# Small experts of a mixture-of-experts layer: more weights split in two, folded and shorter row transfers, and a halved last chunk

## The reference

```
def moe_ffn(h, router_w, router_b, w1, w3, w2):
    logits = h @ router_w + router_b
    top_v, top_i = lax.top_k(logits, 2)
    top_w = jax.nn.softmax(top_v, axis=-1)
    combine = jnp.sum(jax.nn.one_hot(top_i, 8) * top_w[..., None], axis=-2)
    y = jnp.zeros_like(h)
    for e in range(8):
        y = y + combine[..., e:e+1] * swiglu(h, w1[e], w3[e], w2[e])
    return y
```

## Time and profile before

| what | value |
|---|---|
| median of 3 runs (lowest, highest) | 1486.67 us (1479.36, 1486.76) |
| the profiled execution: time, span | 1481.48 us, 1479.8 us |
| granted TensorE clock, mean | 0.993 |
| busy share of the span: PE, DVE, ACT, POOL | 97%, 83%, 64%, 7% |
| moved by DMA | 496 MB, mean 335 GB/s |

### The profile page before, as it was taken

One profiled execution on the slowest core, in us unless ns is written; L12 is line 12 of the kernel. 1 busy time (PEld: TensorE's weight loads), 2 busy tenths in 40 slices (PEclk: granted clock), 3 DMA queues, 4 the chain that ended last, 5 costly groups with the idle time before them and its releaser, 6 DMA issues.

```text
span 1479.8 us, 18836 instructions
## 1 busy us (share of the span) xinstructions
PE 1441.7 (97%) x7449; PEld 1147.2 (78%) x7449; DVE 1233.4 (83%) x1183; ACT 941.4 (64%) x877; POOL 97.8 (7%) x156
## 2 busy tenths in 40 slices
PE   8999999999999999999999999999999999999897
PEld 4886699999988748888887877887867887776674
DVE  5887888887886388998988989888979888988787
ACT  3533444444564247777787877787877787876766
POOL 5400100000000021010000010000010000000000
PEclk9999999999999999999999999999999999999899
DMA  9867588888853349999999999999999999999993
GB/s 348 307 228 284 198 323 320 301 301 303 300 185 115 114 170 333 369 391 379 383 352 374 407 402 410 397 402 409 411 402 409 398 402 409 410 402 410 397 403 154
DMA packets 162436, 496.21 MB, mean 335 GB/s; under 512 B 4650, under 2 KB 8918, under 8 KB 162342
## 3 DMA queue, kind: packets, MB, share of 16 engines
q1 hardware_dynamic: 156160, 474.76, 83.8%
q0 software_dynamic: 5504, 18.78, 3.8%
q10 hardware_dynamic: 678, 1.40, 0.2%
HBM read 483.91 MB, written 11.01 MB: 334 GB/s over the span
## 4 chain that ended last, share of the span: by engine, by line
PE 71%; DMA 12%; DVE 11%; ACT 2%; issue 2%; SPq 1%; POOL 0%; DVEq 0%; ACTq 0%
DMA ring<-in_moe_w_dram 11%; PE bank L1451 9%; PE bank L1452 9%; PE bank L1453 9%; DVE ring_low L2250 6%; PE bank L1091 5%; PE bank L1449 4%; PE bank L1450 4%; PE bank L1299 4%; PE bank L1340 3%; PE bank L1339 3%; PE bank L1338 3%; PE bank L1088 3%; PE bank L1494 2%; PE bank L1314 2%
## 5 line engine op out<-in xcount | busy, mean ns | idle before, releaser
L2250 DVE TENSOR_TENSOR ring_low<-ring,w_high 128x2048 fp32r<-128x2048 f32 x237 | 537.4, 2290 | 53.0 <-ACT w_high L2792 49.4
L2792 ACT ACTIVATE w_high<-ring 128x2048 fp32r<-128x2048 f32 x237 | 451.4, 1920 | 125.2 <-DMA ring<-in_moe_w_dram 60.5
L2250 DVE TENSOR_TENSOR ring_low<-ring,xn_high 128x2048 fp32r<-128x2048 f32 x79 | 180.9, 2289 | 13.7 <-ACT xn_high L2792 11.9
L2705 ACT ACTIVATE tmp_r<-ring 128x1024 fp32r<-128x1024 f32 x84 | 89.0, 1061 | 140.8 <-PE bank L1340 81.9
L1452 PE MATMUL bank<-ring_low,x_high 128*128 128x512 f32 x448 | 175.8, 392 | 0.0
L2792 ACT ACTIVATE xn_high<-ring 128x2048 fp32r<-128x2048 f32 x79 | 151.3, 1915 | 33.7 <-DMA ring<-in_moe_w_dram 18.7
L1450 PE MATMUL bank<-ring_low,x_high 128*128 128x512 f32 x400 | 156.9, 392 | 0.0
L1451 PE MATMUL bank<-w_high,x_high 128*128 128x512 f32 x336 | 133.3, 397 | 0.0
L2046 DVE TENSOR_TENSOR ring_low<-ring,tmp_r 128x1024 fp32r<-128x1024 f32 x84 | 102.6, 1225 | 34.7 <-ACT tmp_r L2705 33.0
L1453 PE MATMUL bank<-w_high,x_low 128*128 128x512 f32 x336 | 131.1, 390 | 0.0
L1449 PE MATMUL bank<-w_high,x_high 128*128 128x512 f32 x304 | 124.2, 408 | 4.7 <-DVE ring_low L2250 3.9
(11 more groups left out here) (448 smaller groups left out, 2619.3 us busy)
## 6 DMA issues: line engine op xcount, KB each, us to landing
ring<-in_moe_w_dram SPq DMA_DIRECT2D x168, 2048.0 KB, 17.1
ring<-in_w_mod_dram SPq DMA_DIRECT2D x23, 2048.0 KB, 13.0
ring<-in_ffn_w_dram SPq DMA_DIRECT2D x21, 2048.0 KB, 11.8
ring<-in_w_in_dram SPq DMA_DIRECT2D x7, 2048.0 KB, 14.1
ring<-in_w_out_dram SPq DMA_DIRECT2D x4, 2048.0 KB, 8.5
ring<-in_w_in_dram SPq DMA_DIRECT2D x4, 1024.0 KB, 15.5
expert_rows<-act_low POOLq DMA_DIRECT2D x5, 512.0 KB, 6.1
ring<-in_w_mod_dram SPq DMA_DIRECT2D x2, 1024.0 KB, 16.1
```

Source lines behind the costliest of these rows:

```text
L2250: tt_(moe_low(u, m // 2)[:, c], moe_slot(u, m // 2)[:, c], high_place(q, g, u, m).bitcast(F32), ALU.subtract).then_inc(low_made, 1)
L2792: act(high_place(q, g, u, m), moe_slot(u, m // 2)[:, c], ACT.Copy).then_inc(high_made, 1)
```

## The change

Four edits:

- `PLAIN` is empty: all units of small experts are split. Only unit 40 of the last expert (`LAST_PLAIN`) stays whole, in `last_down`.
- The last chunk of the last expert is loaded as two transfers of 1 MB with a semaphore each, so that PE can start on unit 40 when its half is there.
- `row_gate` of a small expert adds the two halves of its rows on DVE (two additions of 64 x 512, `fold_v`), and `rows_out` then writes 64 rows by one scatter. The index lists, the adding scatter and the clearing of the spare rows go.
- `tokens_in` gathers 64 rows for small experts, and `turn_rows` transposes 64.

```diff
-PLAIN = (4,16,23,33,39,)
+PLAIN = ()
+LAST_PLAIN = (UNITS - 2,)
...
         def is_plain(q, g, u, m):
-            return is_small(q, g, u) and m in PLAIN
+            return is_small(q, g, u) and (m in PLAIN or (is_last(q, g, u) and m in LAST_PLAIN))
...
-                    eng.dma_start(dst, src).then_inc(landed[(NPRE + c) % RING], 16)
+                    if q == 0 and c == NE * NCH - 1:
+                        eng.dma_start(dst[:, 0:HB // 2, :], src[:, 0:HB // 2, :]).then_inc(s_last_half, 16)
+                        eng.dma_start(dst[:, HB // 2:, :], src[:, HB // 2:, :]).then_inc(landed[(NPRE + c) % RING], 16)
+                    else:
+                        eng.dma_start(dst, src).then_inc(landed[(NPRE + c) % RING], 16)
...
-            for n in range(2 * TT + 1):
+            for n in range(2 * TT):
                 eng.dma_start(expert_rows[n * P:(n + 1) * P, :], y_low.bitcast(F32)).then_inc(s_zero, 16)
...
-                if is_small(0, g, u):
-                    eng.indirect_dma_start(expert_rows[:, :],
...
-                    eng.wait_ge(s_rows_out, 16 * (rows_before(r) + 1))
-                    eng.indirect_dma_start(expert_rows[:, :],
...
-                                           compute_op=ALU.add).then_inc(s_rows_out, 16)
...
+                n = SMALL if is_small(0, g, u) else SLOTS
+                eng.indirect_dma_start(expert_rows[:, :],
+                                       bass.IndirectOffsetOnAxis(index[0:n, g % 2, 0, u, u:u + 1], 0),
+                                       rows_place(r)[0:n, :], None, bounds_check=2 * T + P - 1,
+                                       oob_is_err=False).then_inc(s_rows_out, 16)
...
+                                if is_plain(q, g, u, m):
+                                    ins = mm(bank[4 + half][:, :], act_high[:, j % 2, h].bitcast(F32),
+                                             moe_slot(u, i).rearrange("p (b n) -> p b n", n=D)[:, hb, c],
+                                             start=False, stop=hb == HB - 1)
+                                    continue
...
+                done(eng, tt_(rows[:, c], bank[4 + half][:, :], gate_row[:, c],
+                              ALU.mult).then_inc(fold_v.sem, 1), fold_v, f"y{half}", small_rep(r // PAIR, r % PAIR))
+                done(eng, tt_(rows[0:SMALL, c], rows[0:SMALL, c], rows[SMALL:SLOTS, c],
+                              ALU.add).then_inc(row_v.sem, 1), row_v, f"y{half}", r)
...
-                for u in range(PAIR):
-                    done(eng, tt_(index_f[:, u, PAIR:], index_f[:, u, u:u + 1].to_broadcast([P, 2]), own_rows,
-                                  ALU.max).then_inc(index_v.sem, 1), index_v, f"s{u}", g)
```

More of the change, by code:

```diff
@@ L137 @@
 N_CONSTS = 86
-LATE_CONSTS = 5 + LATER
+LATE_CONSTS = 2 + LATER
 UNUSED = 1000.0
@@ L151 @@
 assert all(COPY_NAMES.index(f"p{j}") < COPY_NAMES.index(f"q{j}") for j in range(NJ))
-SPLITS = [(n, m) for n in range(NE) for m in range(UNITS) if not (n in SMALL_AT and m in PLAIN)]
+LAST_PLAIN = (UNITS - 2,)
+SPLITS = [(n, m) for n in range(NE) for m in range(UNITS)
+          if not (n in SMALL_AT and m in PLAIN) and not (n == NE - 1 and m in LAST_PLAIN)]
 SPLIT = {unit: n for n, unit in enumerate(SPLITS)}
@@ L270 @@
     "index_v":
-        ("f s0 s1 t i").split(),
+        ("f t i").split(),
     "row_v":
+        ("y0 y1").split(),
+    "fold_v":
         ("y0 y1").split(),
@@ L673, in split_at @@
         def split_at(q, g, u, m):
[L675 to L679, removed]
+            if q:
+                return len(SPLITS) + (g * PAIR + u) * UNITS + m + 1
+            return SPLIT[g * PAIR + u, m] + 1
         def high_place(q, g, u, m):
@@ L692, in rows_before @@
         def rows_before(r):
-            return r + sum(is_small(0, n // PAIR, n % PAIR) for n in range(r))
+            return r
         def halves_of(j):
@@ L969, in tokens_in @@
                 for u in range(PAIR):
-                    eng.indirect_dma_start(xn[:, u, :], None, token_rows[:, :],
-                                           bass.IndirectOffsetOnAxis(index[:, g % 2, 1, u, PAIR:PAIR + 1], 0),
+                    n = SMALL if is_small(0, g, u) else SLOTS
+                    eng.indirect_dma_start(xn[0:n, u, :], None, token_rows[:, :],
+                                           bass.IndirectOffsetOnAxis(index[0:n, g % 2, 1, u, PAIR:PAIR + 1], 0),
                                            bounds_check=T - 1, oob_is_err=False).then_inc(s_gathered, 16)
@@ L1401, in turn_rows @@
                         c = k % 2 * T + u * P
-                        ins = nc.tensor.transpose(b[:, c:c + P], xn[:, u, k * P:(k + 1) * P], ident)
+                        rows = SMALL if is_small(0, rep, u) else SLOTS
+                        ins = nc.tensor.transpose(b[:, c:c + rows], xn[0:rows, u, k * P:(k + 1) * P],
+                                                  ident[0:rows, 0:rows])
                 mark(ins.then_inc(gather_t.sem, 1), gather_t, f"g{n}")
@@ L1443, in units_made @@
                         return
-                    moe_arrived(eng, q, g, u, m // 2)
+                    if is_last(q, g, u) and m in LAST_PLAIN:
+                        eng.wait_ge(s_last_half, 16)
+                    else:
+                        moe_arrived(eng, q, g, u, m // 2)
                 def three(out_, x_h, x_l, w_h, w_l, first, last):
@@ L2263, in row_gate @@
                     eng.wait_ge(s_rows_out, 16 * rows_before(r))
-                done(eng, tt_(rows_place(r)[:, half * W:(half + 1) * W], bank[4 + half][:, :], gate_row[:, half * W:(half + 1) * W],
-                              ALU.mult).then_inc(row_v.sem, 1), row_v, f"y{half}", r)
+                c = slice(half * W, (half + 1) * W)
+                rows = rows_place(r)
+                if not is_small(0, r // PAIR, r % PAIR):
+                    done(eng, tt_(rows[:, c], bank[4 + half][:, :], gate_row[:, c],
+                                  ALU.mult).then_inc(row_v.sem, 1), row_v, f"y{half}", r)
+                    return
+                done(eng, tt_(rows[:, c], bank[4 + half][:, :], gate_row[:, c],
+                              ALU.mult).then_inc(fold_v.sem, 1), fold_v, f"y{half}", small_rep(r // PAIR, r % PAIR))
+                done(eng, tt_(rows[0:SMALL, c], rows[0:SMALL, c], rows[SMALL:SLOTS, c],
+                              ALU.add).then_inc(row_v.sem, 1), row_v, f"y{half}", r)
             def indices(g):
```

27 lines of the change are left out of this document (6 added, 21 removed).

## The result

The changed kernel takes 1488.01 us (median of 20 runs, 1480.81 to 1490.90), the kernel before 1480.37 us (20 runs): a ratio of 1.004, with an interval of 1.0031 to 1.005. By this ratio it is slower by 6 us (the medians differ by 7.6), where 10 us less was forecast, and it lies just above the range. The profiled execution took 1486.76 us, with a span of 1484.5 us: 5.3 us more than that of before. Its busy shares are 96% for PE, 86% for DVE, 66% for ACT and 6% for POOL, the clock's mean is 0.990. Executions of one kernel differ with their mean clock: of the changed kernel's 20 the shortest, 1480.81 us, has 0.993, and the longest, 1490.90 us, 0.988.

A forecast was written before the change was run, and what follows sets the result against it. The prediction took the DMA queue to bound the kernel, DVE after the change. 426.4 - 414.2 - 2 = 10.2 us less, +0.4, gave 10 less: 1471.5 on the profiled execution, 1475 us predicted nearer the median's 1476.7, range 1466 to 1487.

The forecast's parts named there:

- I take 2 us for the four together: DVE's remaining waits in small experts 2, 4, 6 and 7: 2 us together, bounds 0 and 28.1.
- The sums of DVE's work: DVE's forecast busy time in small experts 2, 4, 6 and 7 after added subtractions and small edits, together 414.2 us.
- the list of rivals: Alternatives to DVE as bound: queue 0.20, waits unmoved 0.17, SiLU waits staying on top 0.08, slower clock 0.05.
- since PE does not set these stretches: Small experts: PE's 1.6 us less for each of 19 units costs and gains nothing.
- the forecast 12.2 us: Small experts 2, 4, 6 and 7 end 12.2 us earlier if DVE never waits, 414.2 instead of 426.4 us.
- checked the queue at unit 40 and in expert 2: Last weights land 2.6 us ahead of DVE's need; expert 2's copies, checked at units 34 and 40, have as narrow a margin.
- a few tenths at most: Transposes for the next pair: half have 64 columns instead of 128, an effect of a few tenths of a us at most.
- nothing: Ahead of 798 us, beside experts 0 and 1: less clearing, expert 2's shorter gather and fewer constants change nothing.
- The queue, 9.3 us: DMA queue from 820 us: 768 fewer 4 KB rows save 9.3 us, so last weights land at 1447.2 instead of 1456.5.
- taken as 0.4: End of the last expert: unit 40 multiplied whole adds 0.4 us, between 0 and 0.8; the remaining 15.6 us stays.
- The clock rival: Small experts: PE's bursts between subtractions lower its clock; a whole expert at the lower level, 63 us, ends near 1540; chance 0.05.
- The queue stays the bound: Rival: the DMA queue still limits the kernel, 11 us less, 1474 us; chance 0.20.

The follow-up runs named there:

- late_turn: Changed kernel with 128-row transposes and, in small experts, PE's wait for the low part of activation 3 dropped or moved behind unit 27; ratio 0.9996 to kernel before.
- warm_al3: Changed kernel with unused fp32 multiplications on PE ahead of its wait for the low part of activation 3 in small experts; ratio 1.0023 to kernel before.
- late_al3: Changed kernel with PE's wait for the low part of activation 3 dropped or moved behind unit 27 in small experts; ratio 1.0017 to kernel before.
- turn_128: Changed kernel with 128-row transposes for small experts too, gathers staying at 64 rows; ratio 1.0014 to kernel before.
- warm_7: transfers_turn with unused fp32 multiplications on PE ahead of its waits for values 0 and 1 in the last expert; ratio 0.9957 to kernel before.
- best_7: warm_7 with only units 4, 16 and 23 plain among the early units of the last expert; ratio 0.9968 to kernel before.
- split_only: Kernel before with its five plain units per small expert split and nothing else of the change; ratio 1.0034 to kernel before.
- gather_64: Kernel before with only the small experts' gathers cut from 128 to 64 rows, transposes still 128; ratio 0.9998 to kernel before.
- transfers_turn: Changed kernel without its splits (five plain units, unit 40 split, as before) and with 128-row transposes; ratio 0.9967 to kernel before.

## Why the prediction was wrong

**The failed step: "I take 2 us for the four together".** The sums of DVE's work held: 103.3, 103.7, 101.7 and 105.5 us forecast, 103.34, 103.27, 100.94 and 104.62 measured. But the four stretches last 428.4 us instead of 416.2, because DVE was idle for 16.2 us and not for 2. These 12.2 us are most of the miss of 15.3 us between the forecast for the profiled execution, 1471.5, and the 1486.76 measured; 2.0 more lie in the large experts. That term was bounded by the SiLU waits of before, and these did vanish, from 28.1 to 2.1 us. Others took their place, which the list of rivals did not have:

- About 1 us in experts 2 and 4 lies between instructions of a full list (104.15 us for 103.15 busy in late_turn, where DVE has no wait in expert 2), and 2 us in expert 6 (102.75 for 100.78), 1.4 of them waits for ACT; this is left also where the clock holds.
- 0.9 to 1.4 us in each of experts 2, 4 and 6 come from the clock behind PE's wait for the low part of activation 3, shown by warm_al3, late_al3 and expert 4 of turn_128. The prediction called PE's 1.6 us less per unit worth nothing, "since PE does not set these stretches". It had not asked what the shorter PE list reaches sooner.
- The rest is the largest part: expert 7, where DVE was idle for 9.1 us, 6.0 of them waiting for high parts and 1.8 for SiLU. Beside these waits lie two falls of the clock, from 1388 to 1396 us (0.67 and 0.50) after PE had waited 1.2 us for a copy by ACT (`act_m`, L2834), and from 1424 to 1432 us (0.86 and 0.71) at PE's stop of 4.4 us. warm_al3 still has 7.6 us of idle there. No run with all units split took both falls away, as warm_7 did with five units plain, so how much of this is the clock's stays open.

**Where the gain was to come from.** Of the forecast 12.2 us, 11.1 were expert 7's; experts 2, 4 and 6 gave 1.1 together. Expert 7 follows another small expert, so the ring has no large one to refill behind. At 44.04 MB an expert needs 107 to 109 us from the queue, an estimate with the same two rates, more than DVE's 105.5. The changed kernel did not get as far as this limit, since ACT waits for no weights there, but late_turn did: 5.5 us of such waits in its expert 7. The prediction checked the queue at unit 40 and in expert 2, not over the whole of expert 7. Its total, 416.2 + 119.9 + 119.7 = 655.8 us, is 4 us below the shortest of any run (best_7, 659.9).

**The transposes, "a few tenths at most".** They cost 3.9 us in experts 1 and 3 and gave 0.5 in expert 5. That term had no row: only 128-row transposes were in the trace, and two widths side by side not at all. In expert 1 the loss hides. The changed kernel reaches expert 2 at 798.35 us and the kernel before at 798.2, but split_only and gather_64, which have its 128-row transposes in expert 1, get there at 795.6 and 796.4, and turn_128 at 796.1. So the profiled execution of before was about 2 us late at this point, and "nothing" ahead of 798 us was a loss of about 2 us.

**The queue, 9.3 us.** Mechanism and size were nearly right where the splits don't cover it, the source in part not. In transfers_turn the rate falls off and the weights end near 1447.5 us, 651 after the start of expert 2, against 658 before: 7.4 us. The gathers, 192 of the 768 rows and 2.3 of the 9.3 us, give none of it that can be measured; that the scatters give it is argued by elimination, and neither they nor the halved last chunk were tried alone. In the changed kernel DVE and PE free the ring's places later, SP waits for PE, and the queue ends near 1455.5.

**Small terms.** The addition of 64 x 512 takes 0.69 us, taken as 0.68. The tail grew by 0.6, taken as 0.4. The 0.6 us more outside the span were not forecast, and their cause stays open.

**The rivals.** The clock rival had the right sign and a wrong place: not PE's bursts between subtractions, which held 1.00, but single stops of 2.5 to 2.7 us in experts 2, 4 and 6, and a price of 3.6 us there instead of up to 63 (what the falls in expert 7 cost is open). The rule that it drew on (the Trainium skill, TensorE: Matmul & The Clock Gate, A second HAM failure mode: psum-queue depth-cycling) thus gave the direction, but by luck: it tells of frequent short idles, and where PE had those the rows show 1.00 (expert 2 of late_turn, PE busy for 98.29 of 104.15 us). "The queue stays the bound" is what the best versions run into, not this one.

Whether the parts add is not settled: the splits cost 0.0034 on the kernel before, transfers with 128-row transposes give 0.0033, and together (turn_128) they are at 1.0014, but the three intervals are wide enough for a sum of nothing. That the queue's gain is only paid out where no engine fills the stretch is an argument.

## What to carry to other kernels

When work is taken off an engine that is not the bound, look in its list for the next wait that this work covered, and ask what the engine does there, and what its clock does. Before a gain is booked in one stage, hold the new total against every other resource over all stages, bytes over rate first. Where two shapes of one instruction will alternate, a duration from a run of one shape says nothing about them.

## What the runs showed of the hardware

- Transposes of 64 x 64 take 0.08 us each among themselves and those of 128 x 128 0.11, but 0.23 when the two alternate (chain: 0.64, 0.87 and 1.84 us for eight).
- PE stopped for 2.5 us between full activity at 1.00 (expert 6), and the granted clock was 0.78 and 0.79 in the two slices of 4 us from the stop on; two useless fp32 multiplications of 512 columns put into that stop kept it at 1.00, and the stretch was 1.3 us shorter. Not every such stop lets it fall: after 2.7 us in expert 4 of turn_128 it stayed at 1.00.
- One core's queue held 403 GB/s of weights and rows over 620 us with its 16 engines full, and 256 gathered rows of 4 KB less made no difference that can be measured.
